# A two-block transformer kernel: high and low part of x in one product of 512 columns in the second block's FFN

## The reference, cut to what matters

```
def swiglu_ffn(x, g, w_in, w_out):
    h = rms_norm(x, g)
    gate, up = jnp.split(h @ w_in, 2, axis=-1)
    return (jax.nn.silu(gate) * up) @ w_out
...
    x = x + 0.5 * swiglu_ffn(x, ffn1_norm[layer], ffn1_w_in[layer], ffn1_w_out[layer])
```

## Time and profile before

| | us |
|---|---|
| median of 3 runs (2188.81 to 2192.85) | 2189.09 |
| span of the profiled execution | 2186.9 |
| PE busy / DVE busy / ACT busy / POOL busy | 2166.4 / 1509.9 / 1195.7 / 296.7 |
| one `swiglu` stage, about | 188 |

### The profile page before, as it was taken

The page is one execution under the profiler, slowest core; times in us unless marked ns, Lnnn a source line. Parts: engine busy times, 40 slices in busy tenths (PEclk is TensorE's granted clock), DMA queues, the critical chain, the costliest instruction groups (busy, mean ns, idle before and its releaser), DMA issues.

```text
span 2186.9 us, 43460 instructions
## 1 busy us (share of the span) xinstructions
PE 2166.4 (99%) x17612; PEld 2087.2 (95%) x17612; DVE 1509.9 (69%) x2611; ACT 1195.7 (55%) x2060; POOL 296.7 (14%) x273
## 2 busy tenths in 40 slices
PE   9999999999999999999999999999999999999999
PEld 8899989999999999999999999999999999989999
DVE  6767686887578677779856656676656665886654
ACT  5655466665546555566655444455445444665443
POOL 1000112000100011210002210002210220232211
PEclk9999999999999999999999999999999999999999
DMA  7335436355633354455565655345555655435554
GB/s 259 116 126 143 135 109 199 115 176 177 215 120 125 110 153 140 134 166 171 186 196 197 194 184 180 128 129 181 185 189 176 194 184 185 153 118 172 184 186 133
DMA packets 97384, 356.63 MB, mean 163 GB/s; under 512 B 10928, under 2 KB 11056, under 8 KB 97056
## 3 DMA queue, kind: packets, MB, share of 16 engines
q1 hardware_dynamic: 94752, 342.47, 48.6%
q0 software_dynamic: 2000, 10.38, 1.7%
q10 hardware_dynamic: 432, 0.99, 0.1%
HBM read 352.68 MB, written 1.12 MB: 162 GB/s over the span
## 4 chain that ended last, share of the span: by engine, by line
PE 91%; DVE 5%; ACT 2%; issue 1%; DMA 1%; DVEq 0%; ACTq 0%; SPq 0%
PE pd L1364 26%; PE pd L1375 26%; PE pd L1372 25%; DVE wlo L2287 2%; PE pt L1530 1%; PE ps L1364 1%; PE pd L1546 1%; PE ps L1372 1%; PE ps L1375 1%; PE ps L1505 1%; ACT whi L1843 1%; PE ps L1739 1%; PE pd L1652 1%; PE pd L1560 1%; PE ps L1519 1%
## 5 line engine op out<-in xcount | busy, mean ns | idle before, releaser
L1843 ACT ACTIVATE whi<-raw 128x1024 fp32r<-128x1024 f32 x618 | 651.2, 1055 | 601.9 <-PE pd L1375 575.7
L1364 PE MATMUL pd<-xh,whi 128*128 128x256 f32 (+2 forms) x3328 | 973.1, 292 | 1.6 <-DVE tb L2795 1.1
L2287 DVE TENSOR_TENSOR wlo<-raw,whi 128x1024 fp32r<-128x1024 f32 x618 | 768.2, 1244 | 266.6 <-ACT whi L1843 264.6
L1375 PE MATMUL pd<-xh,wlo 128*128 128x256 f32 (+2 forms) x3319 | 941.5, 284 | 0.5 <-DVE wlo L2287 0.4
L1372 PE MATMUL pd<-xl,whi 128*128 128x256 f32 (+2 forms) x3319 | 941.2, 284 | 0.0
L1364 PEld LDWEIGHTS pd<-xh,whi 128*128 128x128 f32 x3328 | 627.6, 189 | 27.1 <-issue 21.0
L1375 PEld LDWEIGHTS pd<-xh,wlo 128*128 128x128 f32 x3319 | 626.2, 189 | 0.9 <-DVE wlo L2287 0.9
L1372 PEld LDWEIGHTS pd<-xl,whi 128*128 128x128 f32 x3319 | 624.7, 188 | 2.4
L1375 PE MATMUL pd<-ah,wlo 128*128 128x256 f32 (+1 forms) x992 | 280.6, 283 | 0.0
L1372 PE MATMUL pd<-al,whi 128*128 128x256 f32 (+1 forms) x992 | 279.6, 282 | 0.0
L1364 PE MATMUL pd<-ah,whi 128*128 128x256 f32 (+1 forms) x992 | 279.3, 282 | 0.0
...
## 6 DMA issues: line engine op xcount, KB each, us to landing
...
```

The lines of the kernel that those rows point to most:

```text
L1364: e.matmul(out, hi, xh, start=begin, stop=False)
L1375: last = e.matmul(out, lo, xh, start=False, stop=end)
L1843: e.activation(m.whi[i][:, 0:n], m.raw[c % NRAW][:, 0:n], ACT.Copy).then_inc(*self.up("ac_hi", ("hi", c)))
L2287: e.tensor_tensor(m.wlo[i][:, 0:n], m.raw[c % NRAW][:, 0:n], m.whi[i][:, 0:n].bitcast(F32), ALU.subtract).then_inc(*self.up("dv_lo", ("lo" ...
```

## The change

It is for stages 4, 6, 7 and 9.

- Behind the first six (stage 4) or three tiles, x is written anew, divided by its root, by the same steps as in `conv_ffn` (`scaled_x`: 8 `z_norm`, 8 `z_hi` and 8 `z_lo`, `z_hi` of k = 0 on DVE). All other `up` tiles are `wide` and use this x; the first three of them run by k.
- A wide block is two matmuls: whi times xh and xl together, 512 columns into the whole bank (the operand is a slice of one tensor `x2`, two runs of 256), and wlo x xh, 256 columns, into the bank's first half.
- When a wide tile leaves PSUM, DVE adds the halves by a `tensor_reduce` over 2 x 256 elements, read as pairs that lie 256 elements apart: `silu_in` for g, a new step `up_add` for v. They are not multiplied by `rs`. POOL then multiplies silu(g) by v (`up_mul`, a new step) in place of `silu_scale`; `silu_up` goes. `act_hi` and `act_lo` are due 0.45 chunks later.
- `xh`/`xl` and `ah`/`al` become halves of `x2` and `a2`. The second product stays as it was, since `WIDE_DOWN` is 0.

```diff
     def swiglu(self, which, l, stage):
...
-        self.await_root(self.dense(order[:n], True, 3))
-        self.dense(order[n:])
+        first = order[:n]
+        for t in order[n:]:
+            t.x, t.wide = "z", True
+        self.await_root(self.dense(first, True, 3))
+        self.last_early.append(first[-1])
+        r0 = self.root_at
+        self.dense(order[n:n + 3], True)
+        self.dense(order[n + 3:])
...
             self.step("dv", g.end + 0.1, "silu_in", stage, g, j)
             self.step("ac", g.end + 0.3, "silu", stage, j)
-            self.step("gp", g.end + 0.5, "silu_scale", stage, j)
-            self.step("dv", s + 0.15, "silu_up", stage, j, v)
-            self.step("ac", s + 0.5, "act_hi", stage, j)
-            self.step("dv", s + 0.8, "act_lo", stage, j)
+            if v.wide:
+                self.hold("tb", s + 0.1, s + 0.9, (stage, j, 1))
+                self.step("dv", s + 0.12, "up_add", stage, j, v)
+                self.step("gp", s + 0.3, "up_mul", stage, j)
+            else:
+                self.step("gp", g.end + 0.5, "silu_scale", stage, j)
+                self.step("dv", s + 0.15, "silu_up", stage, j, v)
+            self.step("ac", s + 0.5 + late, "act_hi", stage, j)
+            self.step("dv", s + 0.8 + late, "act_lo", stage, j)
+        self.scaled_x(stage, r0)
...
+    def scaled_x(self, stage, r0):
+
         for k in range(8):
             self.step("dv", r0 + 0.05 + 0.1 * k, "z_norm", stage, k)
             self.step(*(("ac", r0 + 0.1 + 0.1 * k) if k else ("dv", r0 + 0.04)), "z_hi", stage, k)
             self.step("dv", r0 + 0.17 + 0.1 * k, "z_lo", stage, k)
...
+        if tile.wide:
+            part = m.a2 if tile.x == "a" else m.x2
+            for s in self.ahead(("hi", c), high, low, self.free("pd", tile.key) if begin else None):
+                e.wait_ge(*s)
+            e.matmul(self.buf("pd", tile.key), hi, part[:, :, k, tile.span], start=begin, stop=False)
+            for s in self.ahead(("lo", c)):
+                e.wait_ge(*s)
+            self.block_done(e.matmul(out, lo, xh, start=False, stop=end), c, j)
+            return
...
+    def both(self, dst, t):
+
+        bank = self.buf("pd", t.key)
+        return self.e.tensor_reduce(dst, bank[:, 0:2 * T2].rearrange("p (a b) -> p b a", a=2), AX.X, ALU.add)
...
+    def up_mul(self, stage, j):
+        e = self.e
+        g, v = (self.buf("tb", (stage, j, i))[:, 0:T2] for i in range(2))
+        for s in self.ahead(("silu", stage, j), ("up_add", stage, j)):
+            e.wait_ge(*s)
+        e.tensor_tensor(g, g, v, ALU.mult).then_inc(
+            *self.up("gp_small", ("act", stage, j), ("free", "tb", (stage, j, 1))))
```

More of the change, by code:

```diff
@@ L28 @@
 NMORE, EARLY = 4, 8.0
+WIDE_DOWN = 0
 SBUF_BEGIN, SBUF_END = 16576, 229376
@@ L142, in __init__ @@
         self.begin = self.end = None
+        self.wide = False
 def shifted(by, *spans):
@@ L680, in conv_ffn @@
             self.step("dv", max(s + 1.8, s0 + 2.2), "act_lo", stage, j)
+        self.scaled_x(stage, r0)
+        self.step("ac", d0 + 2.5, "table")
+        self.evac_y(stage, down)
+        self.boundaries.append((int(self.now()), []))
+        self.post_norm(stage, self.now())
+    def scaled_x(self, stage, r0):
         for k in range(8):
@@ L684, in conv_ffn @@
             self.step("dv", r0 + 0.17 + 0.1 * k, "z_lo", stage, k)
-        self.step("ac", d0 + 2.5, "table")
-        self.evac_y(stage, down)
-        self.boundaries.append((int(self.now()), []))
-        self.post_norm(stage, self.now())
     def swiglu(self, which, l, stage):
@@ L694, in swiglu @@
         order, n = [t for p in pairs for t in p], 6 if stage == 4 else 3
-        self.await_root(self.dense(order[:n], True, 3))
-        self.dense(order[n:])
+        first = order[:n]
[6 more added lines that the diff above has]
+        self.dense(order[n + 3:])
         self.flush()
         down = self.tiles(stage, "down", f"{which}_out{l}", 0, 8, NFF, T2, "a")
+        for t in down[:WIDE_DOWN]:
+            t.wide = True
         d0 = self.now()
@@ L705, in swiglu @@
             self.keep("pd", v.key, s + 0.4)
-            self.hold("tb", g.end + 0.1, s + 1.2, (stage, j, 0))
+            late = 0.45 if v.wide else 0.0
+            self.hold("tb", g.end + 0.1, s + 1.2 + late, (stage, j, 0))
             self.step("dv", g.end + 0.1, "silu_in", stage, g, j)
             self.step("ac", g.end + 0.3, "silu", stage, j)
-            self.step("gp", g.end + 0.5, "silu_scale", stage, j)
-            self.step("dv", s + 0.15, "silu_up", stage, j, v)
-            self.step("ac", s + 0.5, "act_hi", stage, j)
-            self.step("dv", s + 0.8, "act_lo", stage, j)
+            if v.wide:
[7 more added lines that the diff above has]
+            self.step("dv", s + 0.8 + late, "act_lo", stage, j)
+        self.scaled_x(stage, r0)
         if stage == 4:
@@ L1085, in __init__ @@
         self.top = arena
[L1086 removed]
+        self.a2 = sb("a2", [128, 2, NFF, T1], F32R)
+        self.ah, self.al = self.a2[:, 0], self.a2[:, 1]
         self.C2 = sb("C2", [128, n2])
@@ L1294, in x_unused @@
 def x_unused(plan, stage):
-    return [] if stage == 0 else [("used", plan.final[stage - 1, "z" if STAGES[stage - 1][0] == "conv_ffn" else "x"])]
+    return [] if stage == 0 else [("used", plan.final[stage - 1, "x"]), ("used", plan.final.get((stage - 1, "z"), 0))]
 def conv_place(engine, stage, t):
@@ L1374, in block, with block_done @@
             e.wait_ge(*s)
-        last = e.matmul(out, lo, xh, start=False, stop=end)
-        events = [("dense", tile.key)] if end else []
+        self.block_done(e.matmul(out, lo, xh, start=False, stop=end), c, j)
+    def block_done(self, last, c, j):
+        tile, k = self.p.chunks[c][j]
+        events = [("dense", tile.key)] if k == tile.ks[-1] else []
         if j == len(self.p.chunks[c]) - 1:
@@ L2257, in run @@
             "v_out": self.v_out, "v_turned": self.v_turned,
-            "silu_in": self.silu_in, "silu_mul": self.silu_mul, "gated": self.gated, "merged_lo": self.merged_lo, "a_pad": self.a_pad,
+            "silu_in": self.silu_in, "up_add": self.up_add, "silu_mul": self.silu_mul, "gated": self.gated, "merged_lo": self.merged_lo, "a_pad": self.a_pad,
             "c_pad": self.c_pad, "zero_queries": self.zero_queries, "d_pad": self.d_pad, "lam_dots": self.lam_dots, "lam_sum": self.lam_sum,
@@ L2391, in silu_in @@
             done = [("silu_in", stage, j), ("free", "pd", t.key)]
+        if t.wide:
+            for s in self.ahead(("dense", t.key), *room):
+                e.wait_ge(*s)
+            self.both(dst, t).then_inc(*self.up("dv_out", *done))
+            return
         for s in self.ahead(("dense", t.key), ("rs", stage), *room):
@@ L2394, in silu_in, with up_add @@
         self.normed(dst, self.buf("pd", t.key)[:, t.span], stage, t.span).then_inc(*self.up("dv_out", *done))
+    def both(self, dst, t):
+        bank = self.buf("pd", t.key)
+        return self.e.tensor_reduce(dst, bank[:, 0:2 * T2].rearrange("p (a b) -> p b a", a=2), AX.X, ALU.add)
+    def up_add(self, stage, j, t):
+        e, key = self.e, (stage, j, 1)
+        for s in self.ahead(("dense", t.key), self.free("tb", key)):
+            e.wait_ge(*s)
+        self.both(self.buf("tb", key)[:, 0:T2], t).then_inc(
+            *self.up("dv_out", ("up_add", stage, j), ("free", "pd", t.key)))
     def silu_mul(self, l, t):
@@ L2823, in residual @@
         H = self.m.h[:, n, T1 - T2:T1]
+        bank = self.buf("pd", t.key)
         for s in self.ahead(("dense", t.key)):
             e.wait_ge(*s)
-        e.scalar_tensor_tensor(H, self.buf("pd", t.key)[:, 0:T2], scale, H, ALU.mult, ALU.add).then_inc(
+        if t.wide:
+            e.scalar_tensor_tensor(H, bank[:, T2:2 * T2], scale, H, ALU.mult, ALU.add).then_inc(
+                *self.up("dv_small", ("res_low", stage, n)))
+            for s in self.ahead(("res_low", stage, n)):
+                e.wait_ge(*s)
+        e.scalar_tensor_tensor(H, bank[:, 0:T2], scale, H, ALU.mult, ALU.add).then_inc(
             *self.up("dv_out", ("res", stage, n), ("free", "pd", t.key)))
```

7 lines of the change are left out of this document (4 added, 3 removed).

## The result

The changed kernel takes **2204.0 us** (median of 4 runs, 2203.4 to 2206.2) against 2189.7 us for the kernel before (4 runs beside them, 2188.8 to 2192.9): a ratio of 1.0067, 95% interval 1.0055 to 1.0079. It is slower by 14.3 us. The profiled execution has a span of 2200.8 us in place of 2186.9, 13.9 us more.

A forecast was written before the change was run, and what follows sets the result against it. PE, busy for 99% of the span, was taken as the bound. 2186.9 - 7.6 (columns) + 20.5 (waits) = 2199.8 us of span; with 2.2 us between span and median, 2202.0 us, range 2192 to 2212.

The forecast's parts named there:

- The columns: PE's wide blocks: two matmuls take 349 ns, 5.9 ns less a block; 1288 blocks give back 7.6 us.
- Rival (b): PE's wide blocks: the 512 columns, as two runs, bring nothing; 2209.6 us; chance 0.10.
- (e): PE's wide blocks: a matmul of 512 columns costs hardly more than one of 256; about 2058 us; chance 0.01.
- The first wait: Start of stage 6: `lo(c0+4)` runs only behind all z steps on DVE, so PE waits 3.1 us.
- The second wait: Start of stage 6: `lo(c0+5)` comes behind pair 0's steps, 5.17 us after `lo(c0+4)`; PE waits 2.4 us more.
- rival (d): Stage starts: granted clock falls in waits, free behind the first, 1.7 us behind the second; 2209 us; chance 0.12.
- Stage 4: Start of stage 4: PE waits for z of k = 0, k = 2 and `lo(c0+8)`, 4.0 us in all.
- The constants: Stage 4: chunk c0+12 is loaded late, into the constants' traffic; 1.0 us (0 to 3).
- The steady part costs nothing: Steady part: DVE goes from 64% to 69% busy with the sums added; price 0.
- The price limit of 1.48 us a sum: Steady part: price stays 0 as long as a reduce occupies DVE for less than 1.48 us.
- Rival (c): Steady part: DVE's reduce becomes the bound; at three times an element's price about 2233 us; chance 0.06.
- Rival (a): Stage starts: waits are absorbed; 2181.5 us with both gone (faster, 0.06), 2191.7 with half gone (0.09).

The follow-up runs named there:

- e4: The changed kernel without the z steps: wide products alone, all tiles on the undivided x, POOL multiplying by rs in place of v; 2181.6 us, ratio 0.9965.
- e13: The changed kernel's z steps and tile order, but every block as three matmuls of 256 columns and tiles evacuated as before; 2213.9 us, ratio 1.0114.
- e1: The changed kernel with `lo(c0+4)` moved ahead of the last four z steps on DVE in stages 6, 7 and 9; 2212.0 us, ratio 1.0107.
- e6: The changed kernel with each sum over pairs made twice on DVE; 2213.1 us, ratio 1.0110.
- e10: The changed kernel with z steps spread between the `lo`, and `hi`, table load and first pairs' steps reordered, in stages 4, 6, 7, 9; 2191.0 us, ratio 1.0009.

## Why the prediction was right, step by step

- **The columns.** Predicted 349 ns a block and 7.6 us; measured 349.2 ns and 7.5 us, alone (e4) and in the changed kernel. Two runs of 256 cost what one run of 512 does. Rival (b) is out, and so is (e). (The prediction takes its comparison with the Trainium skill's formula for both widths from the filling; the 118.3 ns for 256 columns are those of the earlier trace rows.)
- **The first wait.** Predicted: `lo(c0+4)` 8.11 us behind the root's end, measured 8.16; PE's wait 3.1 us, measured 3.2. In stage 7 it is 2.2, in stage 9 3.1.
- **The second wait.** Predicted 2.4 us in stage 6; the trace shows only 0.45 there. The sum is right nevertheless, since 1.7 us went to the clock between the waits. That is the part of rival (d) that the prediction called free, and it is free: the time of `lo(c0+5)` is set by DVE. It starts 4.79 us behind `lo(c0+4)`, for 5.17 predicted. The forecast "a second stand of 2.4 us" as such was wrong in its form. What (d) prices behind a second wait didn't come up in the changed kernel; it is seen in stage 7 of e13 (1.7 us) and in e1, where one wait stands alone (1.7 to 3.0 us).
- **Stage 4.** z of k = 0 late by 1.9 us: measured 1.9. k = 2 by 0.5: measured 0.45, and another 0.5 in small pieces. `lo(c0+8)`: 1.6 predicted, 2.25 measured. The constants: 1.0 predicted, 0 measured. The `hi` that they delay stood 1.17 us for its load (before: 4.10), and PE's chunks are 2.79 us apart from c0+9 on; that the waits ahead had given the transfer time is likely and was not tested. So the stage lost 1.5 us more than its terms at the waits and 1.0 less at the constants, and came out at 5.5 for 5.0; that these nearly cancel is luck. ACT in stage 4 of the changed kernel:

```profile
1199.28 1.06 ACT L1878 ACTIVATE whi<-raw 128x1024 fp32r<-128x1024 f32 x1 [1.17 <-DMA raw<-in_w]
```

- **The steady part costs nothing.** Right, though DVE's load was sized too low. The changed kernel in a window of stage 6 (before: the earlier trace rows):

```profile
1520.00:1610.00 90.00, 90.00 (x517) 78.98 (x516) 71.85 (x83) 46.58 (x66) 11.77 (x16) 1.00 0.57 189
```

80% for 69% predicted. The forecast added distances between starts and compared them with a busy share, which counts whole durations where instructions stand apart: 0.08 to 0.09 us for each of a pair's five, up to 6.7 us in 16 pairs. A further 16 x 0.27 = 4.3 us are the `lo` that take 1.50 us. The price limit of 1.48 us a sum was too high as well (e6). Rival (c) is out: the sum takes 0.69 us, far below either limit.
- **Rival (a)**, z cheaper than thought, is out: z step to z step is 0.73 to 0.74 us. Its idea, to run `lo` ahead of z, was half right: e10 brings 11.6 of 20.7 us back and no more.
- **The sum.** -7.5 + 20.7 = 13.2 us, and 0.7 us lies outside these stages' first products. Predicted 12.9.
